# Attention stage of a hybrid encoder layer: 128-row transposes of scaled weights in place of 64-row matmuls with a diagonal, and another order of the table loads

## The reference, cut to what matters

```
# memory: 4 heads of 64, 256 keys
s = einsum('bshd,bmhd->bhsm', q, k) * HEAD_DIM ** -0.5
p = softmax(s, axis=-1)
y = einsum('bhsm,bmhd->bshd', p, v)
# neighbourhood: 8 heads; a query of the 16 x 64 token grid sees a window of 8 x 16 keys
s = einsum('bqhd,bnqmhd->bhqnm', q_r, k_nb) * scale + bias
p = softmax(s.reshape(B, H, GRID_W, kh * NA_KW), axis=-1)
y = einsum('bhqnm,bnqmhd->bqhd', p, v_nb)
```

## Time and profile before

| | |
|---|---|
| median of three executions | 1177.3 us |
| profiled execution, its time | 1179.72 us |
| its span in the trace | 1178.0 us |
| TensorE matmul busy | 1119.1 us, 95% |
| TensorE weight load busy | 617.2 us, 52% |
| VectorE, ScalarE, GpSimd busy | 538.9, 306.2, 252.2 us |
| mean granted clock of TensorE | 0.981 of full speed |
| attention stage | 402.8 to about 524.5 us |

### The profile page before, as it was taken

The page is one execution under the profiler, slowest core; times in us unless marked ns, Lnnn a source line. Parts: engine busy times, 40 slices in busy tenths (PEclk is TensorE's granted clock), DMA queues, the critical chain, the costliest instruction groups (busy, mean ns, idle before and its releaser), DMA issues. The chain is left out here.

```text
span 1178.0 us, 24178 instructions
## 1 busy us (share of the span) xinstructions
PE 1119.1 (95%) x9610; PEld 617.2 (52%) x9610; DVE 538.9 (46%) x1285; ACT 306.2 (26%) x797; POOL 252.2 (21%) x350
## 2 busy tenths in 40 slices
PE   6999999999999888987989999999999999999997
PEld 5534444444444457666985455664444444455553
DVE  4349526799969453654673444563111111111111
ACT  5054123622231364763561212300000000000000
POOL 0300410030000131522350001242445511112211
PEclk9989999999999995999999999999999999999999
DMA  9540343151220495425744841369999999767433
GB/s 339 172 83 26 102 143 87 36 179 35 91 63 36 115 198 109 137 68 135 216 130 180 278 188 73 115 231 411 425 349 347 378 331 363 287 268 294 147 118 123
DMA packets 126750, 218.13 MB, mean 185 GB/s; under 512 B 55428, under 2 KB 90724, under 8 KB 122744
## 3 DMA queue, kind: packets, MB, share of 16 engines
q1 hardware_dynamic: 101512, 135.44, 34.2%
q0 software_dynamic: 17216, 49.84, 12.5%
q10 hardware_dynamic: 7920, 31.46, 7.8%
HBM read 184.92 MB, written 40.82 MB: 192 GB/s over the span
## 5 line engine op out<-in xcount | busy, mean ns | idle before, releaser
L528 PE MATMUL pj_ps<-hT,pj_w 128*128 128x512 f32 x576 | 253.5, 596 | 0.0
L528 PEld LDWEIGHTS pj_ps<-hT,pj_w 128*128 128x128 f32 x576 | 108.1, 190 | 135.7 <-issue 135.1
L1589 PE MATMUL ps_out<-w_out,mixT 128*128 128x512 f32 x256 | 112.3, 594 | 2.0 <-PEq L2823 1.7
L2435 PE MATMUL ex_py<-wd,ex_hT 128*128 128x512 f32 x256 | 113.1, 592 | 0.0
L740 DVE RECIPROCAL mixT<-mixT 128x1024 f32<-128x1024 f32 (+1 forms) x11 | 68.9, 6262 | 23.9 <-ACT mixT L660 18.9
L2584 ACT ACTIVATE ex_sg<-ex_pg 128x512 f32<-128x512 f32 x16 | 9.6, 597 | 269.5 <-PE ex_pg L2489 269.5
L1589 PEld LDWEIGHTS ps_out<-w_out,mixT 128*128 128x128 f32 x256 | 47.9, 190 | 59.4 <-issue 59.4
L2503 PE MATMUL ex_pu<-proj 128*128 128x512 f32 x176 | 78.2, 592 | 0.0
L2489 PE MATMUL ex_pg<-proj 128*128 128x512 f32 x176 | 77.6, 594 | 0.0
L2435 PEld LDWEIGHTS ex_py<-wd,ex_hT 128*128 128x128 f32 x256 | 47.1, 190 | 52.8 <-issue 52.8
L2698 DVE TENSOR_TENSOR ex_hid<-ex_pu,ex_sg 128x512 f32<-128x512 f32 x16 | 11.1, 692 | 136.2 <-PE ex_pu L2503 136.2
(11 more groups left out here) (365 smaller groups left out, 1902.3 us busy)
## 6 DMA issues: line engine op xcount, KB each, us to landing
wd<-in_moe_w_down ACTq DMA_DIRECT2D x15, 2048.0 KB, 9.8
proj<-in_moe_w_gate SPq DMA_DIRECT2D x11, 2048.0 KB, 10.9
proj<-in_moe_w_up SPq DMA_DIRECT2D x11, 2048.0 KB, 11.7
mixT<-in_moe_w_gate SPq DMA_DIRECT2D x5, 2048.0 KB, 11.0
mixT<-in_moe_w_up SPq DMA_DIRECT2D x5, 2048.0 KB, 10.0
pj_w<-in_w_in SPq DMA_DIRECT2D x18, 512.0 KB, 4.1
proj<-in_x SPq DMA_DIRECT2D x16, 512.0 KB, 10.3
products<-pj_unit POOLq DMA_DIRECT2D x4, 2048.0 KB, 9.9
```

The source lines that it names most:

```text
L528: mm = pe.matmul(ps[:, t % 2, half, :], w_tile(t)[:, n, :], s.hT[:, n, half * 512:(half + 1) * 512], start=(n == 0), stop=(n == KD - 1))
L1589: mm = pe.matmul(s.ps_out[:, t % 2, half * 512:(half + 1) * 512], s.mixT[:, k, t * P:(t + 1) * P], s.w_out[:, k, half * 512:(half + 1) * 5 ...
L2435: mm = pe.matmul(py[:, half, :], hT[:, j, :], wd[e % 2][:, j, half * 512:(half + 1) * 512], start=(j == 0), stop=(j == KF - 1))
```

## The change

The weights are scaled in place by VectorE, one `tensor_scalar` for each R, in place of the multiply into `diag`; `diag` is gone, and with it the wait for `turned`. `scaled` counts two for each step. The turn is a TensorE transpose with the 128x128 identity: one for each two pieces (128 keys) and both heads at once; the last one of an odd number of pieces has 64 keys. The turned weights of the two heads lie side by side in 64 columns each, so `at_ps_t` and `at_ptb` lose their bank-for-head axis, `BASE[1]` is 256 columns, and `weigh` reads other offsets; its products are the same ones. The copy has as many columns as before. SyncE loads the tables first and then does the lay-out, factors 2 and the inverses 0 to 2.

```diff
-BASE = [0, 2 * HALF_P]
+BASE = [0, 2 * P]
...
-        ptb = sb("ptb", [P, 2, 2, 320])
+        ptb = sb("ptb", [P, 2, 5 * P])
...
-        diag = sb("diag", [P, 2, 2, HALF_P])
...
-        ps_t = c.enter_context(nc.psum_tensor("at_ps_t", [P, 2, 512], F32))
+        ps_t = c.enter_context(nc.psum_tensor("at_ps_t", [P, 2 * 512], F32))
...
             for i in range(2):
                 load_factors(sp, s, i)
-            sp.wait_ge(s.full_zeroed, 32)
-            lay_out_inverses(sp, s)
-            sp.wait_ge(s.laid_out, LAID_OUT)
-            load_inverses(sp, s, 0)
             n = 0
             for v in (LEFT, RIGHT, MID):
...
-            sp.wait_ge(scored, len(MEMORY_STEPS))
+            sp.wait_ge(s.full_zeroed, 32)
+            lay_out_inverses(sp, s)
             load_factors(sp, s, 2)
-            for i in range(1, 3):
+            sp.wait_ge(s.laid_out, LAID_OUT)
+            for i in range(3):
                 load_inverses(sp, s, i)
...
             def turn(k):
-                pe.wait_ge(scaled, k + 1)
+                pe.wait_ge(scaled, 2 * k + 2)
                 pe.wait_ge(pt_ready, k) if k else pe.wait_ge(zeroed, 2)
                 for R in range(2):
-                    for a in range(pieces(k, R)):
-                        o0 = a % 2 * HALF_P
-                        for b in range(2):
-                            p0, p1 = b * HALF_P, (b + 1) * HALF_P
-                            mm = pe.matmul(ps_t[o0:o0 + HALF_P, b, BASE[R] + a // 2 * HALF_P:BASE[R] + (a // 2 + 1) * HALF_P],
-                                           pr(k, R)[p0:p1, k % 3, a * HALF_P:(a + 1) * HALF_P], diag[p0:p1, k % 2, R, :], start=True, stop=True)
+                    for a in range(-(-pieces(k, R) // 2)):
+                        keys = min(P, pieces(k, R) * HALF_P - a * P)
+                        mm = pe.transpose(ps_t[0:keys, BASE[R] + a * P:BASE[R] + (a + 1) * P], pr(k, R)[:, k % 3, a * P:a * P + keys], s.ident)
                 mm.then_inc(turned, 1)
...
             for b in range(2):
-                dve.memset(ps_t[:, b, 0:320], 0.0).then_inc(zeroed, 1)
+                dve.memset(ps_t[:, b * 512:(b + 1) * 512], 0.0).then_inc(zeroed, 1)
...
-                if k >= 2:
-                    dve.wait_ge(turned, k - 1)
-                dve.tensor_tensor(diag[:, k % 2, :, :], s.fold.unsqueeze(1).to_broadcast([P, 2, HALF_P]),
-                                  inv[:, k % 2, :].unsqueeze(2).to_broadcast([P, 2, HALF_P]), ALU.mult).then_inc(scaled, 1)
+                for R in range(2):
+                    part = pr(k, R)[:, k % 3, 0:keys_of(k, R)]
+                    dve.tensor_scalar(part, part, inv[:, k % 2, R:R + 1], None, ALU.mult).then_inc(scaled, 1)
...
-                    cols = BASE[1] + -(-pieces(k, 1) // 2) * HALF_P
-                    act.activation(ptb[:, k % 2, :, 0:cols], ps_t[:, :, 0:cols], ACT.Copy).then_inc(pt_ready, 1)
+                    cols = BASE[1] + -(-pieces(k, 1) // 2) * P
+                    act.activation(ptb[:, k % 2, 0:cols], ps_t[:, 0:cols], ACT.Copy).then_inc(pt_ready, 1)
```

More of the change, by code:

```diff
@@ L1072, in weigh @@
                         for h in range(2):
-                            at, step = (0, BASE[1] + 320) if h == 0 else (BASE[1], 320 - BASE[1])
-                            both = ptb[:, k % 2, :, :].rearrange("p s c -> p (s c)")[:, at + a * HALF_P:]
+                            at, step = (0, BASE[1] + HALF_P) if h == 0 else (BASE[1], HALF_P - BASE[1])
+                            both = ptb[:, k % 2, at + a * P:]
                             both = bass.AP(both.tensor, both.offset, [both.ap[0], [step, 2], [1, HALF_P]])
@@ L1089, in weigh @@
                             mm = pe.matmul(ps_o[h * HD:(h + 1) * HD, k % 2, R * HALF_P:(R + 1) * HALF_P], v,
-                                           ptb[0:rows, k % 2, slot(R, h), BASE[R] + a * HALF_P:BASE[R] + (a + 1) * HALF_P],
+                                           ptb[0:rows, k % 2, BASE[R] + a * P + slot(R, h) * HALF_P:BASE[R] + a * P + (slot(R, h) + 1) * HALF_P],
                                            start=(a == 0), stop=(a == last - 1))
```

## The result

The changed kernel takes 1202.05 us, median of six executions (1197.48 to 1203.68), against 1175.45 (1172.98 to 1180.02) for the kernel before: ratio 1.0217, 95% interval 1.0188 to 1.0247. It is slower, where 1161.2 and a gain were forecast.

The account below looks back on a forecast made before the run. The attention stage was taken to bound gains, its steps set by a cross-engine loop plus stops from late code. Stops 15.0 + turn 1.1 = 16.1 us off 1179.7 gave 1163.6 profiled, 1161.2 median; range 1156 to 1174.

Parts of the forecast that it names:

- the first part: Opening account of what bounds the kernel: attention stage, 402.8 to about 524.5 us, on one chain; 15.0 us lost to disturbance.
- Part 2: TensorE code in attention: 40 or 66 instructions a step for 96 or 128, so all 15.0 us of stops go.
- Rival D: Slower, chance 0.10: granted clock might not hold with transposes in attention, near steps at 1.2 GHz, +13 us, 1190.
- 1. Turn on TensorE: Attention's turn as transposes: 0.05 us less per loop of two steps, 24 loops, 1.1 us gained; bounds -1.3 to 4.4.
- 3. VectorE: Attention: two tensor_scalars at 0.35 us replace a 0.29 multiply; round 1.8, at most 2.1, under the 2.27 loop; no cost.
- case E: VectorE becomes the bound in attention: 24 wide steps lose 0.13 each, 3.1 us: 1164; chance 0.05.
- 4. ScalarE's copy: Attention's copy keeps its 512 or 640 columns, in one run, so no change; the larger memset finishes in time.
- 5. SyncE: Attention's loads: tables in the first 20 steps, lay-out at about 440, inverses by about 471; cost nothing.
- B: Code still comes late once in attention's near steps, giving back up to 12.3 us: 1164 to 1173.5; chance 0.18.
- C: Attention's stops have another cause and stay, only the loop moves: 1176.2; chance 0.09.
- The sum: Whole program: 15.0 + 1.1 = 16.1 us less, 1179.7 to 1163.6 profiled, 1161.2 as median; chance 0.58.

## Why the prediction was wrong

**The step that failed** is one sentence of the first part: "nothing of the next stage starts before it ends, so what it gains the program gains". As far as semaphores and the barrier go it is true: the scan starts 1.8 us after the attention's end, as it did before (1.7). But the stages share one more thing: TensorE's code is one row of instructions, and what is taken out moves all that stands behind it. So the scan's time, which the sum carried over unchanged, was not given. Part 2 counted how much code the change removes, and used the number for the attention alone. The same 2704 instructions moved the scan's loop from place 66 to 178, and that costs 35.7 us. No rival named it. Rival D, the one on the slow side, got 1190 for another reason that did not occur; its nearness to 1202 is worth nothing.

The rows to see the danger were there. Queue 8 has 12 packets over the scan of the kernel before. The scan has 3072 matmuls and 3072 weight loads, 24 packets of 256, if all of it were fetched (written out it needed 25). Twelve is only possible if two of the loop's three rounds need none. The view that gave for the attention, asked for the scan, would have shown that the scan lives on a resident loop. That the place decides it could not be read from one trace, but it could have been a rival with a price: the fetching rate in that loop.

**Part by part.**
1. Turn on TensorE. Forecast a waiting turn of 0.58 and 0.69, measured 0.55 and 0.67; two memory steps 4.06 against 4.08 forecast, a wide step 2.23 against about 2.25. Against 4.13 and 2 x 2.27 before that is 0.07 to 0.08 a loop, 24 loops give about 1.8 for 1.1. The choice of a first load that is not hidden was right.
2. Code supply. The attention is 14.8 us shorter where 16.1 were summed, and the instructions and packets came as counted. That all of the gain is late code is not shown. The 15.0 us were priced from one execution. The stage with the old code and the old order took 121.3, 113.8, 114.8, 122.9 and 122.9 in the five kernels that have both, and the 114.8 is from a kernel that differs from before only behind the attention. Three of the five lost 3.1 to 3.5 us to the wait of the first near step and not to a long stop inside a turn. The stage with the new code and the new order took 105.6 to 106.5 in all six. Half the code with the old order gives 109.1, the new order with all the code 111.1. By the ratios the order alone is worth 5.9 us, half the code alone 8.9, both together 12.9 (8.3 to 17.5), and the intervals leave open whether the two add up. I had put the table order at nothing, and it brings a gain. The lasting gain of the change is better read from the ratio 0.989, 13 us of 1175.
3. VectorE. 355 and 356 ns a piece against 0.35, no turn released by the scaling: case E did not occur.
4. ScalarE's copy still releases the turns, as before.
5. SyncE. Tables from 401.68, lay-out from 438.69, inverses out by 463.75: about as forecast (405, 440, 471), at no cost.

**Rivals.** B: no late code inside the attention's turns. C: the stops inside turns are gone. That is as late code would be, but the longest of them, 2.92 us, is also missing in three of four other kernels with the old code and order, so the cause of the stops in the earlier trace rows is not settled. D: the granted clock is 0.97 over the attention with all its transposes. The Trainium skill, page "TensorE: Matmul & The Clock Gate", section "Part 4: PE-mode transpose", says that a transpose does not count as a busy engine; in a stage where other matmuls stand between the transposes, there is no fall of the clock behind the start of the stage.

**The sum** of the forecast, without the loop's place: 1163.6 for the profiled execution. The version with its loop back in a good place took 1166.06 in its profiled execution (span 1164.3), and its median is 1163.19 against 1161.2. That the median comes within 2.0 us is in part luck: the 15.0 us for the stops were one execution's, and the causes of the gain were not those of part 2 alone. What was missing from the forecast for the changed kernel is one term, 131.0 - 94.3 = 36.7 us.

## What to carry to other kernels

- If a change adds or removes instructions on an engine, look for every loop behind it on that engine, and compare the packets of the code queue there with the instructions that it executes. Fewer packets than instructions / 256 means a loop that runs from resident code, and its place becomes a cost of any edit ahead of it.
- Where a stage grows that the diff does not touch, ask the code queue before the data queues; moving the loop by one slot (no work added) is a cheap test and may be the remedy.
- Where a change cuts both code and transfers in a stretch, run each part alone before the gain is put down to either, and compare medians: one profile of the kernel before had 121.3 us for a stage that took 113.8 and 114.8 in others.

## What was not expected of the hardware

- The place of a loop of 1644 TensorE instructions, modulo 256, changes its stage from 93.5 to 131.0 us, with values in between (107.1 to 114.4).
- A jump back to code that is no longer there stops TensorE for 5.87 and 5.90 us (5.2 to 6.4 over all kernels), and pieces of half clock follow: the mean granted clock of the scan is 0.86 against 1.00.
- Code that is fetched straight on, without a jump, also costs: 115.0 against 94.3 us, where a slot of the scan has about 100 instructions in 1.4 us.
- Always-met waits on TensorE cost 0.11 us for each instruction that they become (28.92 - 14.92 = 14.0 us for 128).
